# Up projections of a feed-forward phase: from one 512-column and one 256-column product to three 256-column products into one sum

## What is computed

```python
D_MODEL, SEQ, D_FF = 1024, 256, 2816

def swiglu(h, w13, w2):
    a, g = jnp.split(h @ w13, 2, axis=-1)
    return (jax.nn.silu(a) * g) @ w2

for l in range(DEPTH):                       # first stack; the second norms the block's result too
    x = x + 0.5 * swiglu(rms_norm(x, ffn1_norm[l]), ffn1_w13[l], ffn1_w2[l])
    ...
    x = x + 0.5 * swiglu(rms_norm(x, ffn2_norm[l]), ffn2_w13[l], ffn2_w2[l])
```

## Time and profile before

| | |
|---|---|
| median of 3 runs | 3809.09 us (3804.3 to 3820.05) |
| span of the profiled execution | 3803.0 us |
| TensorE busy | 3455.1 us, 91% |
| VectorE busy | 2200.5 us, 58% |
| ScalarE busy | 1822.4 us, 48% |
| mean granted clock of TensorE | 0.920 |
| read from memory | 615.62 MB, 164 GB/s over the span |

### The profile page before, as it was taken

One profiled execution on the slowest core, in us unless ns is written; L12 is line 12 of the kernel. 1 busy time (PEld: TensorE's weight loads), 2 busy tenths in 40 slices (PEclk: granted clock), 3 DMA queues, 4 the chain that ended last, 5 costly groups with the idle time before them and its releaser, 6 DMA issues.

```text
span 3803.0 us, 49605 instructions
## 1 busy us (share of the span) xinstructions
PE 3455.1 (91%) x17816; PEld 2948.4 (78%) x17816; DVE 2200.5 (58%) x2348; ACT 1822.4 (48%) x2295; POOL 111.2 (3%) x256
## 2 busy tenths in 40 slices
PE   7987889999779899998999978889999899998899
PEld 6876778888677787877787867778787678787787
DVE  5565555555655555566556573655556655656555
ACT  4454445444555444445444443444445544445444
POOL 0000000000000000000000000100000000000000
PEclk9988999999889999997999986689999889999699
DMA  6653345545333454543454542235454345444254
GB/s 235 216 186 113 126 155 188 188 178 188 137 122 126 157 197 166 183 176 112 171 191 171 187 147 104 85 142 179 176 188 171 127 144 196 176 180 172 84 197 167
DMA packets 105044, 618.35 MB, mean 163 GB/s; under 512 B 10816, under 2 KB 19008, under 8 KB 34656
## 3 DMA queue, kind: packets, MB, share of 16 engines
q1 hardware_dynamic: 84288, 562.07, 41.0%
q10 hardware_dynamic: 20640, 54.71, 4.4%
HBM read 615.62 MB, written 9.50 MB: 164 GB/s over the span
## 4 chain that ended last, share of the span: by engine, by line
PE 80%; DVE 9%; ACT 6%; issue 2%; DVEq 1%; POOL 1%; DMA 1%; ACTq 1%; POOLq 0%
PE ps L1304 32%; PE ps L1308 16%; PE ps L1368 6%; PE ps L1367 6%; PE ps L1369 6%; PE ps L1467 2%; PE ps L1325 2%; PE ps L1327 2%; PE ps L1326 2%; DVE wlo L863 2%; PE ps L1343 2%; ACT whi L557 2%; PE ps L1456 1%; ACT pr L733 1%; DVE s L1041 1%
## 5 line engine op out<-in xcount | busy, mean ns | idle before, releaser
L1304 PE MATMUL ps<-xhl,whi 128*128 128x512 f32 x5216 | 1837.6, 402 | 41.9 <-DVEq L378 39.8
L863 DVE TENSOR_TENSOR wlo<-raw,whi 128x2048 fp32r<-128x2048 f32 x526 | 1204.0, 2292 | 840.1 <-ACT whi L557 840.1
L1308 PE MATMUL ps<-xhl,wlo 128*128 128x256 f32 x5216 | 1364.4, 282 | 0.0
L1304 PEld LDWEIGHTS ps<-xhl,whi 128*128 128x128 f32 x5216 | 959.0, 191 | 236.5 <-issue 48.0
L557 ACT CAST whi<-raw 128x2048 fp32r<-128x2048 f32 x526 | 999.2, 1903 | 261.5 <-PE ps L1369 128.0
L1308 PEld LDWEIGHTS ps<-xhl,wlo 128*128 128x128 f32 x5216 | 1003.1, 192 | 58.7
L1368 PE MATMUL ps<-wlo,ht 128*128 128x512 f32 x1056 | 417.2, 395 | 0.0
L1367 PE MATMUL ps<-whi,ht 128*128 128x512 f32 x1056 | 417.1, 395 | 0.0
L1369 PE MATMUL ps<-whi,ht 128*128 128x512 f32 x1056 | 416.7, 395 | 0.0
L630 ACT COPY tg<-ps 128x512 f32<-128x512 f32 x132 | 77.5, 587 | 431.0 <-PE ps L1304 431.0
L1369 PEld LDWEIGHTS ps<-whi,ht 128*128 128x128 f32 x1056 | 198.3, 188 | 48.0
(11 more groups left out here) (196 smaller groups left out, 3175.5 us busy)
## 6 DMA issues: line engine op xcount, KB each, us to landing
raw<-stream SPq DMA_DIRECT2D x528, 1024.0 KB, 4.8
bias<-rel_bias ACTq DMA_DIRECT2D x80, 256.0 KB, 2.6
gain<-gains ACTq DMA_DIRECT2D x19, 1024.0 KB, 4.7
bias<-fixed_bias ACTq DMA_DIRECT2D x40, 256.0 KB, 2.7
rel_bias<-rel_vectors SPq DMA_DIRECT2D x16, 512.0 KB
x<-x_tokens ACTq DMA_DIRECT2D x1, 1024.0 KB, 4.9
y_tokens<-x ACTq DMA_DIRECT2D x1, 1024.0 KB, 3.9
cst<-constants ACTq DMA_DIRECT2D x1, 670.0 KB, 6.7
```

What stands on the lines that cost most here:

```text
L863: nc.vector.tensor_tensor(wlo[:, slot, :], raw[:, slot, :], whi[:, slot, :].bitcast(F32), ALU.subtract).then_inc(sem["lo_ready"], 1)
L1304: wide = lambda: pe.matmul(ps[:, bank, 0:2 * half], hi[:, k, col0:col0 + P], src[:, k0 + k, :], start=first and k == 0, stop=last and k == ...
L1308: e = pe.matmul(ps[:, bank, 0:half], lo[:, k, col0:col0 + P], src[:, k0 + k, 0:half], start=False, stop=False)
```

## The change

An up step no longer calls `feature_tile`. For each of its two tiles it issues for each k three 256-column products into the same 256 columns: high weights by high activations, high weights by low activations, low weights by high activations. The two tiles of a step lie side by side in one bank (bank 0 for `a`, bank 2 for `g`). ScalarE takes silu straight from bank 0, and VectorE multiplies bank 2 by `silu` straight to `h`. The tiles `ta`, `a_sum`, `tg` and `g_sum` and their four instructions for each pair are gone, with their semaphores. TensorE may overwrite bank 0 after `silu_ready` of the pair before, and bank 2 after `h_ready` of the pair before. VectorE waits for `step_used` of the `g` step itself, and ScalarE waits before silu for `h_ready` of the pair before, since `h` reads `silu`. The order of the weights, their steps and their splits stay as they are, and so do projections and gates.

In the diff the first part is ScalarE's, the second VectorE's, the last two TensorE's.

```diff
             def ffn(ph):
                 def half_a(j):
-                    nc.scalar.copy(ta[:, :, :], ps[:, 0:2, 0:T]).then_inc(sem["low_a"], 1)
-
-                    act.wait_ge(sem["a_summed"], j + (base(ph, "a_summed") + 1))
-                    nc.scalar.activation(silu[:, :, :], a_sum[:, :, :], ACT.Silu).then_inc(sem["silu_ready"], 1)
+
+                    if not isinstance(j, int) or j > 0:
+                        act.wait_ge(sem["h_ready"], j + base(ph, "h_ready"))
+                    nc.scalar.activation(silu[:, :, :], ps[:, 0, :].rearrange("p (a b) -> p a b", a=2),
+                                         ACT.Silu).then_inc(sem["silu_ready"], 1)
 
                 def half_g(j, buffer=0):
-                    nc.scalar.copy(tg[:, :, :], ps[:, 2:4, 0:T]).then_inc(sem["low_g"], 1)
                     act.wait_ge(sem["h_ready"], j + (base(ph, "h_ready") + 1))
                     nc.scalar.copy(ht[:, buffer, :, 0, :], h[:, :, :]).then_inc(sem["hh_ready"], 1)
...
             def ffn(ph):
-                def half_a(j):
-                    dve.wait_ge(sem["low_a"], j + (base(ph, "low_a") + 1))
-                    if not isinstance(j, int) or j > 0:
-
-                        dve.wait_ge(sem["silu_ready"], j + base(ph, "silu_ready"))
-                    nc.vector.tensor_tensor(a_sum[:, :, :], ps[:, 0:2, T:2 * T], ta[:, :, :], ALU.add)\
-                        .then_inc(sem["a_summed"], 1)
-
-                def half_g(j, buffer=0):
-                    dve.wait_ge(sem["low_g"], j + (base(ph, "low_g") + 1))
-                    nc.vector.tensor_tensor(g_sum[:, :, :], ps[:, 2:4, T:2 * T], tg[:, :, :], ALU.add)\
-                        .then_inc(sem["g_summed"], 1)
-                    dve.wait_ge(sem["g_summed"], j + (base(ph, "g_summed") + 1))
+                def half_g(c, j, i=None, stride=0, buffer=0):
+                    dve.wait_ge(sem["step_used"], at_step(c + 1, i, stride))
                     dve.wait_ge(sem["silu_ready"], j + (base(ph, "silu_ready") + 1))
 
                     if not isinstance(j, int) or j > 0:
                         dve.wait_ge(sem["ht_ready"], j + base(ph, "ht_ready"))
-                    nc.vector.tensor_tensor(h[:, :, :], g_sum[:, :, :], silu[:, :, :], ALU.mult)\
+                    nc.vector.tensor_tensor(h[:, :, :], ps[:, 2, :].rearrange("p (a b) -> p a b", a=2), silu[:, :, :],
+                                            ALU.mult)\
                         .then_inc(sem["h_ready"], 1)
...
                 def up(c, bank, j=None):
 
                     use(c, j, 3)
-                    w = step_parts(c, KD, 2 * P)
-                    feature_tile(bank, w, 0, xhl)
-                    feature_tile(bank + 1, w, P, xhl).then_inc(sem["step_used"], 1)
+                    hi, lo = step_parts(c, KD, 2 * P)
+                    for tile in range(2):
+                        dst = ps[:, bank, tile * T:(tile + 1) * T]
+                        cols = slice(tile * P, (tile + 1) * P)
+                        for k in range(KD):
+                            pe.matmul(dst, hi[:, k, cols], xhl[:, k, 0:T], start=k == 0, stop=False)
+                            pe.matmul(dst, hi[:, k, cols], xhl[:, k, T:2 * T], start=False, stop=False)
+                            e = pe.matmul(dst, lo[:, k, cols], xhl[:, k, 0:T], start=False, stop=k == KD - 1)
+                    e.then_inc(sem["step_used"], 1)
...
                 def body(j, c, i=None, first=False):
 
-                    pe.wait_ge(sem["a_summed"], j + base(ph, "a_summed"))
+                    pe.wait_ge(sem["silu_ready"], j + base(ph, "silu_ready"))
                     up(c, 0, i)
                     down(c + 1, j - 1, i, first=first)
-                    pe.wait_ge(sem["g_summed"], j + base(ph, "g_summed"))
+                    pe.wait_ge(sem["h_ready"], j + base(ph, "h_ready"))
                     up(c + 2, 2, i)
```

More of the change, by code:

```diff
@@ L164, in ffn @@
         add("ffn", ("pe", "act", "dve"), 3 * n,
-            up=dict(low_a=n, low_g=n, a_summed=n, g_summed=n, silu_ready=n,
+            up=dict(silu_ready=n,
                     h_ready=n, hh_ready=n, ht_ready=n, acc_half=1))
@@ L317, in transformer_stacks @@
             [("chl", [P, 5, 2 * T], F32R)])
-        (low_half, logits, gate, part_sum, merged, ta, a_sum, silu, tg, g_sum, h, ht, tl, whole, high, cblk, chid, cpre, scmp, s, pr, pt, qs, qps, bias) = overlay(
+        (low_half, logits, gate, part_sum, merged, silu, h, ht, tl, whole, high, cblk, chid, cpre, scmp, s, pr, pt, qs, qps, bias) = overlay(
             [("low_half", [P, 2, 2, T], F32), ("logits", [P, 2, 2, T], F32), ("gate", [P, 2, 2, T], F32),
              ("part_sum", [P, 2, 2, T], F32), ("merged", [P, 2, 2, T], F32)],
-            [("ta", [P, 2, T], F32), ("a_sum", [P, 2, T], F32), ("silu", [P, 2, T], F32), ("tg", [P, 2, T], F32),
-             ("g_sum", [P, 2, T], F32), ("h", [P, 2, T], F32), ("ht", [P, 2, 2, 2, T], F32R)],
+            [("silu", [P, 2, T], F32), ("h", [P, 2, T], F32), ("ht", [P, 2, 2, 2, T], F32R)],
             [("tl", [P, 2, 2, T], F32), ("whole", [P, 2, 2, T], F32), ("high", [P, 2, 2, T], F32R), ("cblk", [P, LP, KVG, NCMP], F32), ("chid", [P, 2, 2, NBLK], F32),
@@ L977, in ffn @@
                 split(ph.step + 2)
-                half_a(0)
                 split(ph.step + 3)
-                half_g(0)
+                half_g(ph.step + 1, 0)
                 with dve.Fori(1, PAIRS - 1) as j:
                     split(ph.step + 1, j, 3)
-                    half_a(j)
                     split(ph.step + 2, j, 3)
                     split(ph.step + 3, j, 3)
-                    half_g(j)
+                    half_g(ph.step + 1, j, j, 3)
                 split(end - 2)
-                half_a(PAIRS - 1)
                 split(end - 1)
-                half_g(PAIRS - 1, 1)
+                half_g(end - 3, PAIRS - 1, buffer=1)
                 split(end)
@@ L1387, in ffn @@
                 last, end = PAIRS - 1, ph.step + 3 * PAIRS
-                pe.wait_ge(sem["a_summed"], last + base(ph, "a_summed"))
+                pe.wait_ge(sem["silu_ready"], last + base(ph, "silu_ready"))
                 up(end - 4, 0)
-                pe.wait_ge(sem["g_summed"], last + base(ph, "g_summed"))
+                pe.wait_ge(sem["h_ready"], last + base(ph, "h_ready"))
                 up(end - 3, 2)
```

## The result

| | before | after |
|---|---|---|
| median of the runs | 3812.9 us (4 runs, 3804.3 to 3820.1) | 3848.3 us (4 runs, 3847.9 to 3849.1) |
| ratio, after to before | | 1.0094, 95% interval 1.0074 to 1.0113 |
| span of the profiled execution | 3803.0 us | 3846.2 us |

The change makes the kernel slower by 0.9%, 35 us by the medians. The two spans differ by 43.2 us. In every run that is listed with both, the span lies 1.7 to 1.9 us under the time, so the profiled execution of before, with its span of 3803.0 us, was one of about 3805 us and among the fastest.

A forecast was written before the change was run, and what follows sets the result against it. TensorE's unbroken stream of products was taken to bound the feed-forward phases. Removed work 0, added products 4170 x 0.0096 = 40 us, on a median of 3809 us gives 3849 us; range 3822 to 3872 us.

The forecast's parts named there:

- What is removed: Two ScalarE copies and two VectorE adds per feed-forward pair, beside products TensorE never waits on: worth 0.
- What is added: Up steps: one more product with its own weight load for each k, 4224 in all, columns unchanged at 768.
- The price: Up steps: three 256-column products take 0.3593 us against 0.3497 now, 0.0096 us more for each k.
- The sum: Whole kernel: 4170 k at full clock times 0.0096 us, 40 us longer.
- under 10 us: Half-clock stretches at the feed-forward phases' edges: twelve starts shifted by a few us should leave under 10 us.
- The lower bound: Up steps: each further product costs only 4 ns, 17 us in all.
- the line: Through token-tile products of 352 and 512 columns in the earlier trace: 0.000446 us for a column, 0.004 us for a product.
- The direct measure: Row of 256-column products in the earlier trace's `kv` token tiles: 0.1198 us each, three make 0.3593 us.
- the cadence of two narrow neighbours: Rival for the up steps: all narrow products run at 0.115 us, 20 us faster, 3789 us; chance 0.05.
- The rule of the Trainium skill: Warm product costs its columns at 2.4 GHz plus some 2.5 ns: 11 us more, 3820 us; not in the sum.
- a product within the loop takes 0.125 us: Rival for the up steps: loads or operand reads collide with the splits, 107 us slower, 3916 us; chance 0.08.

The follow-up runs named there:

- the split with the old epilogue: Kernel before, only each 512-column product of an up step made two of 256 columns, copies and adds kept: 3849.8 us, ratio 1.0090.
- The 288-column products: Kernel before with three 288-column products for each k of the up steps in place of 512 and 256: 4003.0 us, ratio 1.0509.
- the uneven split: Kernel before, up steps' 512-column product of each k but the first split into 320 and 192 columns: 3910.3 us, ratio 1.0266.
- the split down step: Kernel before with each 512-column product of the down steps made two of 256, except four per phase: 3830.7 us, ratio 1.0045.

## Why the prediction was right

**The median** was forecast at 3849 us and is 3848.3. Part of that fit is luck of the runs: the forecast was 40 us on a median of 3809.1, and the difference of the medians with one more run of before is 35 us, that of the spans 43 us.

**What is removed is worth 0**: shown, to within the interval. The old products with the new epilogue take the time of before (0.9995, 0.9985 to 1.0004), and in the changed kernel TensorE waits for nothing new. The step that it rested on, that a busy engine with no waits in the earlier trace rows can't gain from others' relief, is the one to repeat.

**What is added, 4224 products with loads of their own**: shown by the counts and by the split with the old epilogue (1.0090), which alone gives the loss.

**The price, 0.0096 us for a k**: measured 0.3597 - 0.3497 = 0.0100 us in the up steps, and at 0.3593 the estimate of a k from the token tiles of the earlier trace rows was within 0.0004 us. The down step gives 0.017 us of a pair back, for which the forecast had no term, so what a pair pays is 0.301 us, 0.0094 us for a k. That the roles of weights and activations are exchanged there was taken to be of no weight. It was not quite so: the down steps' row was at 0.1187 us. The `kv` tiles have exchanged roles too and were at 0.1198, so what differs isn't the roles alone.

**The sum, 40 us**: from the start of each phase's first up product to its last down product, the twelve phases took 2233.5 us before and 2272.2 us after, added up from the starts in the two traces; that is 38.7 us. A phase that ran wholly at full clock took 184.5 us before (1832.59 to 2017.08 us) and 187.8 after (2058.74 to 2246.54 us). The 4.5 us that remain of the 43.2 lie between the phases, where nothing was changed; there the profile of after has 586 us at half clock and that of before 572. The forecast had under 10 us for that.

**The lower bound** (4 ns for a product, from the earlier trace rows) was too low as a price. The 288-column products lie at 0.1325 us and the 352-column ones of the earlier trace rows at 0.1610: 0.445 ns for a column, 4 ns for a product, as the line said. At 256 columns that gives 0.1183 us; the down steps show 0.1187, and the up steps' 0.1199 lies 0.0016 us above it, three times for each k. So the price of a k in the up steps, 10 ns, is one product's 4 ns, some 5 ns because the narrow row in an up step lies above the line, and 1 ns because the wide and narrow pair of before (0.3497 us) lay just below it (768 x 0.000445 + 2 x 0.0044 = 0.3506). The direct measure had the first two in it, the line only the first. Why a row of 256 columns lies above the line is open.

**The rivals.** That the cadence of two narrow neighbours (0.115 us) would hold in a row fell: 0.1199 us over 96. The rule of the Trainium skill ("TensorE: Matmul & The Clock Gate", section "Wait — 56ns, not 53.3ns?"), some 2.5 ns for a product beyond its columns, would by that estimate have made 11 us; the chip paid 35. In this kernel's type and with a load for every product, a 256-column product takes 0.119 to 0.120 us in a row of its like and not the page's 109 ns, so the measurement decides. That a product within the loop takes 0.125 us because loads or reads are in the way (3916 us) fell for 256 columns, but the uneven split shows how near it was: with 192 columns in the row the kernel takes 3910 us.

## What to carry to other kernels

Where an engine is busy without a wait, ask what a change does to that engine's own stream, in starts from one product to the next; relief for the others is worth nothing until a wait shows that they are late. Splitting a 512-column product into two of 256 keeps the columns and still cost 6 to 10 ns each time here, and a product under 240 columns cost as much as one of 240, most likely because its weight load no longer hid under it. The best estimate of a new pattern's price here was the same pattern elsewhere in the same trace. And the price of a change is read over a whole period of the loop: a dozen products of the split down step give 0.1183 us each, its 48 give 0.1187, and the pair shows a cost in the unchanged products beside them as well.

## What was not expected of the hardware

With a load before each product, the distance between starts was 0.112 us at 48, 192 and 240 columns alike, then 0.1187 to 0.1199 at 256 and 0.1325 at 288. The floor holds for each product by itself: 320, 192 and 256 columns took 0.377 us together and three times 256 took 0.360. And the delay that a too short product causes shows one product later, between the starts of the next two.
